# RWKV features and scan: idle products ahead of waits, decay jobs in head pairs, bonus products between the gates', three VectorE operations per key chunk, and one GpSimd operation fewer per unit

## What is computed

```python
u = _centred_token_shift(u, mu).astype(f32)
r, k, v, wd, ad, gd = jnp.split(u, splits, axis=-1)
w = -jax.nn.softplus(-(w0 + jnp.einsum('bldr,drc->bldc', jnp.tanh(wd), w2))) - 0.5
decay = jnp.exp(-jnp.exp(w))
a = jax.nn.sigmoid(a0 + jnp.einsum('bldr,drc->bldc', ad, a2))
g = jax.nn.sigmoid(gd) @ g2
kk = (k * k_k).reshape(B, L, H, N)
kk = kk / jnp.maximum(jnp.sqrt(jnp.sum(kk * kk, axis=-1, keepdims=True)), 1e-12)
k_dir = k[:, :, None, :] * (1.0 + (a - 1.0) * k_a)
...
_, ys = lax.scan(_rwkv7_step, S0, seq)          # the scan, both directions
...
bonus = jnp.sum(r_h[:, :, None] * k_h * r_k, axis=-1, keepdims=True)
y = y + (jnp.sum(bonus, axis=2) * v_h).reshape(B, L, D_RWKV)
y = y * g
return y.astype(out_dtype) @ w_o
```

## Time and profile before

| | before |
|---|---|
| median of 3 runs (lowest, highest) | 3057.55 us (3047.7, 3060.89) |
| the profiled execution: its own time | 3049.9 us |
| its span, first to last instruction | 3048.1 us |
| PE busy | 2815.7 us, 92% of the span |
| DVE, ACT, POOL busy | 1561.3, 871.8, 376.5 us |
| clock granted to TensorE, mean over the span | 0.961 of full speed |
| the features stage | about 508.5 to 551.2 us of the span |
| the scan | about 551.2 to 841 us |

### The profile page before, as it was taken

How to read it: one execution, slowest core, us unless ns; L and a number is a source line. 1 busy time by engine, 2 the same in 40 slices (tenths; PEclk the granted TensorE clock), 3 DMA queues, 4 the chain that set the end, 5 groups by cost and what they waited for, 6 DMA issues and landing times. The chain is left out here.

```text
span 3048.1 us, 40943 instructions
## 1 busy us (share of the span) xinstructions
PE 2815.7 (92%) x17635; PEld 2216.8 (73%) x17635; DVE 1561.3 (51%) x2138; ACT 871.8 (29%) x1119; POOL 376.5 (12%) x356
## 2 busy tenths in 40 slices
PE   7999999788899999999999999799999669999997
PEld 6888876577765777788887854578887545688886
DVE  5555454566676734555545317463354545463342
ACT  3222234211134223322213423332222334432221
POOL 1111010211110001111100001121121100120110
PEclk9999999899999999999999988899999879999999
DMA  4555531000030023355544210223343200222321
GB/s 146 169 169 162 163 114 50 2 3 3 3 119 14 28 83 97 110 163 169 164 161 126 89 43 0 70 69 105 110 145 104 56 31 29 70 83 97 97 97 55
DMA packets 267444, 272.05 MB, mean 89 GB/s; under 512 B 12751, under 2 KB 248246, under 8 KB 267071
## 3 DMA queue, kind: packets, MB, share of 16 engines
q1 hardware_dynamic: 251904, 207.57, 22.0%
q0 software_dynamic: 15360, 61.87, 6.2%
HBM read 267.32 MB, written 2.10 MB: 88 GB/s over the span
## 5 line engine op out<-in xcount | busy, mean ns | idle before, releaser
L915 DVE TENSOR_TENSOR mix_wl<-ring_raw,mix_wh 128x2048 fp32r<-128x2048 f32 (+2 forms) x66 | 153.1, 2320 | 220.1 <-ACT mix_wh L807 220.0
L707 PE MATMUL mix_ps<-h_mix_hi,mix_wh 128*128 128x512 f32 x624 | 244.1, 391 | 0.0
L709 PE MATMUL mix_ps<-h_mix_lo,mix_wh 128*128 128x512 f32 x624 | 242.8, 389 | 0.0
L807 ACT ACTIVATE mix_wh<-ring_raw 128x2048 fp32r<-128x2048 f32 (+2 forms) x66 | 117.6, 1782 | 212.5 <-PE mix_ps L713 162.1
L707 PE MATMUL ffn_ps<-h_rw_hi,ffn_wh 128*128 128x512 f32 x448 | 175.3, 391 | 0.0
L709 PE MATMUL ffn_ps<-h_rw_lo,ffn_wh 128*128 128x512 f32 x448 | 174.3, 389 | 0.0
L915 DVE TENSOR_TENSOR mlp_wl<-ring_raw,mlp_wh 128x2048 fp32r<-128x2048 f32 (+1 forms) x38 | 96.7, 2545 | 131.5 <-ACT mlp_wh L807 131.5
L915 DVE TENSOR_TENSOR mlp_wl<-mlp_raw,mlp_wh 128x2048 fp32r<-128x2048 f32 x36 | 93.2, 2589 | 133.3 <-ACT mlp_wh L807 133.3
L713 PE MATMUL mix_ps<-h_mix_hi,mix_wl 128*128 128x512 f32 x624 | 154.2, 389 | 0.0
L707 PE MATMUL mlp_ps<-view,mlp_wh 128*128 128x512 f32 x384 | 150.1, 391 | 0.0
L709 PE MATMUL mlp_ps<-view,mlp_wh 128*128 128x512 f32 x384 | 149.5, 389 | 0.0
(11 more groups left out here) (589 smaller groups left out, 6210.4 us busy)
## 6 DMA issues: line engine op xcount, KB each, us to landing
ring_raw<-in_mlp_w SPq DMA_DIRECT2D x32, 1024.0 KB, 5.3
mlp_raw<-in_mlp_w SPq DMA_DIRECT2D x32, 1024.0 KB, 5.2
ffn_sraw<-in_ada_w POOLq DMA_DIRECT2D x34, 768.0 KB, 5.1
ffn_raw<-in_ffn_w_gu SPq DMA_DIRECT2D x44, 512.0 KB, 5.1
ring_raw<-in_ffn_w_gu SPq DMA_DIRECT2D x44, 512.0 KB, 4.8
mix_sraw<-in_ada_w POOLq DMA_DIRECT2D x22, 768.0 KB, 5.0
ring_raw<-in_w_in SPq DMA_DIRECT2D x14, 1024.0 KB, 5.2
ring_raw<-in_a_w_in SPq DMA_DIRECT2D x12, 1024.0 KB, 5.2
```

What stands on the lines that cost most here:

```text
L707: nc.tensor.matmul(ps[:, it.banks[t], :], w(h, k, t), xh[:, k, :], start=it.first and k == it.k0, stop=False)
L709: nc.tensor.matmul(ps[:, it.banks[t], :], w(h, k, t), xl[:, k, :], start=False, stop=False)
L807: nc.scalar.activation(slot(wh, it), slot(raw, it), ACT.Copy).then_inc(hi_ready, 1)
L915: nc.vector.tensor_tensor(slot(wl, it), slot(raw, it), slot(wh, it).bitcast(F32), ALU.subtract)\
```

## The change

It has six parts.

1. In the features, PE issues six `keep_clock` products between the first four jobs and the spread, once the square root is ready (`n_root`).
2. The decay jobs go chunk by chunk, both directions next to each other, as the `a` jobs did already.
3. Each bonus product stands behind its chunk's gate job and not behind all jobs.
4. DVE makes r * r_k * k for all chunks (`krr`) ahead of the reciprocal, and then has three operations per chunk, not four: s = a_fwd + a_bwd - 2; s * k_a * krr; 2 * krr + that.
5. A table `rest` = 1 - k_a is made once, and GpSimd's factor is a * k_a + rest in one pass: the operation over all 512 columns that added 1.0 (L1944) goes, with its wait.
6. At the scan's start PE waits for `logs_done`, issues six `keep_clock` products, makes unit 0's `begin`, and issues six more.

```diff
@@ rwkv_features
+        krr = sb("krr", [P, RT, L])
+        kd, rk = sb("kd", [P, L]), sb("rk", [P, 2, L])
@@
         jobs = [("a", d, c) for c in range(RT) for d in range(2)] + \
-               [("w", d, c) for d in range(2) for c in range(RT)] + [("g", 0, c) for c in range(RT)]
+               [("w", d, c) for c in range(RT) for d in range(2)] + [("g", 0, c) for c in range(RT)]
@@ tensor
                 if n == 4:
+                    pe.wait_ge(n_root, 1)
+                    keep_clock(nc, e, pn[:, RT - 1, :], 6)
                     pe.wait_ge(spread_in, 16)
                     pe.wait_ge(inv_ready, 1)
@@
-            for c in range(RT):
-                pe.wait_ge(rk_ready, c + 1)
-
-                pe.wait_ge(kk_ready, c + 1)
-                nc.tensor.matmul(pn[:, c, :], e.heads[:, :], rk[:, c % 2, :], start=True, stop=True)\
-                    .then_inc(b_done, 1)
+                if kind == "g":
+                    pe.wait_ge(rk_ready, c + 1)
+                    pe.wait_ge(kk_ready, c + 1)
+                    nc.tensor.matmul(pn[:, c, :], e.heads[:, :], rk[:, c % 2, :], start=True, stop=True)\
+                        .then_inc(b_done, 1)
@@ vector
             pick_heads(nc, e, dve, pick, picked)
+            ka = COL["rw_k_a"]
+            nc.vector.tensor_scalar(grown, e.cols[:, ka:ka + RT], -1.0, 1.0, ALU.mult, ALU.add)
+            for c in range(RT):
+                st.mark(nc.vector.scalar_tensor_tensor(krr[:, c, :], r[:, c, :], col(e, "rw_r_k", c), k[:, c, :],
+                                                       ALU.mult, ALU.mult))
+            dve.wait_ge(steps, st.n)
             dve.wait_ge(n_root, 1)
@@
-                then(nc.vector.tensor_scalar(kd[:, 0, :], kd[:, 0, :], col(e, "rw_k_a", c), 2.0,
-                                             ALU.mult, ALU.add))
-                then(nc.vector.tensor_tensor(kd[:, 0, :], kd[:, 0, :], k[:, c, :], ALU.mult))
+                then(nc.vector.scalar_tensor_tensor(kd[:, :], kd[:, :], col(e, "rw_k_a", c), krr[:, c, :],
+                                                    ALU.mult, ALU.mult))
                 if c >= 2:
                     dve.wait_ge(b_done, c - 1)
-                nc.vector.scalar_tensor_tensor(rk[:, c % 2, :], kd[:, 0, :], col(e, "rw_r_k", c), r[:, c, :],
-                                               ALU.mult, ALU.mult).then_inc(rk_ready, 1)
+                nc.vector.scalar_tensor_tensor(rk[:, c % 2, :], krr[:, c, :], 2.0, kd[:, :], ALU.mult, ALU.add)\
+                    .then_inc(rk_ready, 1)
@@ rwkv_scan, gpsimd
                 for c in range(RT):
-                    ins = nc.gpsimd.tensor_scalar(kd[:, c, :], au[:, c, :], -1.0, col(e, "rw_k_a", c), ALU.add, ALU.mult)
+                    ins = nc.gpsimd.tensor_scalar(kd[:, c, :], au[:, c, :], col(e, "rw_k_a", c), col_at(rest, c),
+                                                  ALU.mult, ALU.add)
                 ins.then_inc(kd_done, 1)
-                pool.wait_ge(kd_done, 4 * u + 1)
-                nc.gpsimd.tensor_scalar(kd[:, :, :], kd[:, :, :], 1.0, None, ALU.add).then_inc(kd_done, 1)
-                pool.wait_ge(kd_done, 4 * u + 2)
+                pool.wait_ge(kd_done, 3 * u + 1)
@@ tensor
+            pe.wait_ge(logs_done, 1)
+            keep_clock(nc, e, pc[0], 6)
             begin(0)
+            keep_clock(nc, e, pc[0], 6)
```

More of the change, by code:

```diff
@@ L1721, in load_spread, with rwkv_features @@
     return sp.dma_start(spread[:, :, :], I["c_sel"].rearrange("k (h p) -> k h p", h=2 * RT)[:, :, 0:CH])
-def rwkv_features(nc, e, I, rkv, lora, lw, a, g, kk, bonus, tables):
+def rwkv_features(nc, e, I, rkv, lora, lw, a, g, kk, bonus, grown, tables):
     r, k, v = rkv[:, 0:RT, :], rkv[:, RT:2 * RT, :], rkv[:, 2 * RT:3 * RT, :]
@@ L1740, in rwkv_features @@
         pick, spread = sb("pick", [P, RT, 2 * RT]), sb("spread", [2 * RT, 2 * RT, CH])
-        kd = sb("kd", [P, 2, L])
-        rk = sb("rk", [P, 2, L])
+        krr = sb("krr", [P, RT, L])
+        kd, rk = sb("kd", [P, L]), sb("rk", [P, 2, L])
         ps = pb("ps", [P, 4, L])
@@ L1845, in _ @@
                 dve.wait_ge(taken, 2 * c + 2)
-                then(nc.vector.scalar_tensor_tensor(kd[:, 0, :].rearrange("p (q i) -> p q i", i=QL), a[:, 0, :, c, :], -2.0,
+                then(nc.vector.scalar_tensor_tensor(kd[:, :].rearrange("p (q i) -> p q i", i=QL), a[:, 0, :, c, :], -2.0,
                                                     a[:, 1, :, c, :], ALU.add, ALU.add))
-                then(nc.vector.tensor_scalar(kd[:, 0, :], kd[:, 0, :], col(e, "rw_k_a", c), 2.0,
-                                             ALU.mult, ALU.add))
-                then(nc.vector.tensor_tensor(kd[:, 0, :], kd[:, 0, :], k[:, c, :], ALU.mult))
+                then(nc.vector.scalar_tensor_tensor(kd[:, :], kd[:, :], col(e, "rw_k_a", c), krr[:, c, :],
+                                                    ALU.mult, ALU.mult))
                 if c >= 2:
                     dve.wait_ge(b_done, c - 1)
-                nc.vector.scalar_tensor_tensor(rk[:, c % 2, :], kd[:, 0, :], col(e, "rw_r_k", c), r[:, c, :],
-                                               ALU.mult, ALU.mult).then_inc(rk_ready, 1)
+                nc.vector.scalar_tensor_tensor(rk[:, c % 2, :], krr[:, c, :], 2.0, kd[:, :], ALU.mult, ALU.add)\
+                    .then_inc(rk_ready, 1)
                 dve.wait_ge(rk_ready, c + 1)
@@ L1871, in level_columns, with rwkv_scan @@
     return t.rearrange("p m (g two b) -> p (m g) two b", two=2, b=b)[:, :, odd, :]
-def rwkv_scan(nc, e, I, rkv, lw, a, kk, y, g, bonus, reset, scan_mask, levels):
+def rwkv_scan(nc, e, I, rkv, lw, a, kk, y, g, bonus, rest, reset, scan_mask, levels):
     r, k, v = rkv[:, 0:RT, :], rkv[:, RT:2 * RT, :], rkv[:, 2 * RT:3 * RT, :]
@@ L2225, in scale @@
                 elif part == 2:
-                    dve.wait_ge(kd_done, 4 * u + 4)
+                    dve.wait_ge(kd_done, 3 * u + 3)
                     if u >= 2:
@@ L2451, in rwkv_branch @@
         reset, mask, levels = sb("reset", [P, L]), sb("mask", [P, 2, P]), sb("levels", [P, 2 * LEVELS + 1, CH])
+        rest = sb("rest", [P, RT])
         tables = [(reset[:, :], I["c_reset"]), (mask[:, :, :], I["c_scan"].rearrange("p (d t) -> p d t", d=2)),
                   (levels[:, :, :], I["c_levels"].rearrange("p (k t) -> p k t", t=CH))]
-        rwkv_features(nc, e, I, rkv, y, lw, a, g, kk, bonus, tables)
-        rwkv_scan(nc, e, I, rkv, lw, a, kk, y, g, bonus, reset, mask, levels)
+        rwkv_features(nc, e, I, rkv, y, lw, a, g, kk, bonus, rest[:, :], tables)
+        rwkv_scan(nc, e, I, rkv, lw, a, kk, y, g, bonus, rest, reset, mask, levels)
     return bonus, g
```

## The result

| | before | changed |
|---|---|---|
| median (lowest, highest) of 7 runs each | 3057.52 us (3047.7, 3060.89) | 3037.65 us (3029.84, 3040.91) |
| the profiled execution: its own time | 3049.9 us | 3036.13 us |

The ratio is 0.9937, with a 95% interval of 0.9922 to 0.9951. Measured once more (after_again, five runs against nine of before), the same kernel came to 3038.32 against 3051.3 us, 0.9950 (0.9933 to 0.9968). The forecast was 3042 (3030 to 3053) and a gain of 13.5; the medians give 19.9 and 13.0.

A forecast was written before the change was run, and what follows sets the result against it. PE sets the features' end; in the scan its waits for `scaled` and `x` lie on the path. Gains 6.1 + 2.1 + 5.3 = 13.5 give 3036.4 us from the profiled execution, 3044 from the median; said 3042, range 3030 to 3053.

The forecast's parts named there:

- first rival: Whole kernel: the clock gains more, through the shorter wait for x in the units; about 3035 us, chance 0.22.
- spread behind idle products: Features, PE: with six idle products in the gap the spread takes about 4.6 us, not 7.16; gain 2.4.
- second four `a` jobs: Features, PE behind the spread: left at the lower clock, gain 0, up to 1.4 if the clock does not fall.
- decay jobs: Features, PE: eight jobs with alternating row halves take 4.3 us instead of 5.72; gain 1.4 (0.9 to 1.7).
- gates and bonus products: Features, PE: 12.65 us without a stall instead of 14.35, since `rk` is early; gain 1.7.
- tail: End of features, DVE: only the last product with v follows PE, 1.33 us becomes 0.7; gain 0.6.
- up to the reciprocal (`krr`): Features: four `krr` operations, 3.0 us, fit in DVE's idle 5.60 ahead of `n_root`; cost 0.
- scan's start: Scan's first unit: 0.5 from GpSimd's lost pass and 1.6 from the idle products' clock; gain 2.1 (-1 to 4.7).
- units 1 to 6: Scan: `kka` ends before L2248, which falls to 0.68 us; `x` comes 0.88 earlier six times, gain 5.3.
- second rival: Features: GpSimd blocks DVE for a whole pass, fourth `krr` ends at 517.85; gain 10.8, 3047 us, chance 0.10.
- slack of 0.45: Scan's units 1 to 6: GpSimd's four small operations may cost 0.1 us more each with their second table before it goes.
- third rival: Scan's units: small operations slower, `kka` still meets L2248; gain 8.2, 3050 us, or 3053 if idle products cover nothing; chance 0.13.

The follow-up runs named there:

- a_early_kd: Changed kernel with GpSimd's four unit 0 operations made in the features, unit 1's waiting for unit 0's x, idle products 4 and 5; 3035.88 us, 0.9942 of before.
- a_jobs_old: Changed kernel with the decay jobs by direction again, equal row halves next to each other; single time 3039.14 us.
- a_four_ops: Changed kernel with VectorE's four operations per chunk again and no r * r_k * k ahead of the reciprocal; single time 3036.43 us.
- a_pool_old: Changed kernel with GpSimd's five old operations per unit, the pass that adds 1.0 being back; 3046.08 us, 0.9987 of before.
- b_pool_new: Kernel before with GpSimd's new operations alone, the small table made by VectorE in the features; 3049.13 us, 0.9988 of before.
- b_pool_late: Kernel before with GpSimd's old operations, the next unit's waiting for x of the present one (started in place of scaled); 3046.95 us, 0.9985 of before.
- a_no_idle_feat: Changed kernel without the features' six idle products, those at the scan's start staying; no time given, 30.39 us from reciprocal to scan against 28.44 changed.
- a_no_idle: Changed kernel without its eighteen idle products, in the features and at the scan's start; 3038.68 us, 0.9964 of before.

## Why the prediction was right

The time lies in the range and the gain has the forecast's sign; the terms held less well than their sum. The first medians' gain, 19.9, lies beyond the forecast's 10 to 17, in a part (over 15.3) to which I had given 0.40; the second measurement's 13.0 and the traces' 16.1 lie within 10 to 17. By time alone 3037.65 is as near to the first rival's 3035 as to 3042; the lengths of the units decide between them. The trace of before is that of a fast execution, 7.6 under the median. Step by step, in us gained:

| step | said | the traces |
|---|---|---|
| spread behind idle products | 2.4 | 3.5 |
| second four `a` jobs | 0 | 0.5 |
| decay jobs | 1.4 | 0.5 |
| gates and bonus products | 1.7 | 2.2 |
| tail | 0.6 | 0.6 |
| up to the reciprocal (`krr`) | 0 | -0.7, of which `krr`'s -0.3 |
| scan's start | 2.1 | 2.5 |
| units 1 to 6 | 5.3 | 5.3, and 1.6 of the clock's |
| sum | 13.5 | 16.1 |

The **spread** was sized by the group norm's row, in which the clock fell half way; here it held to the end, and the next job starts 3.6 after the spread does, the upper bound that I gave and did not take. It fell behind the spread instead, in the `a` jobs, and stayed down into the first decay jobs.

**Decay jobs**: these eight took 5.26 and not the 4.3 that I had sized, and the clock is the small part of the miss. In a_early_kd it stood at 1.00 through all of them, and they still took 5.10, from 525.84 to 530.94: seven steps of 0.58, each job starting 0.05 behind the end of one of ScalarE's operations, and 1.05 from the last job to the first gate. So ScalarE, which frees the buffers of `ps` every 0.58, sets the pace of the pairs. I had that case, 4.8 if it binds throughout, and did not take it, because the four buffers let PE run ahead; it binds all the same. By direction TensorE's own 0.72 is the slower of the two, which is why pairing is worth 0.8 (a_jobs_old) and not 1.4. **Gates and bonus products** are 12.12 and not 12.65, as the products next to a bonus product follow after 0.96 and not 1.06.

**krr**: GpSimd's pass did not block VectorE. The four took 3.08, 0.77 each, beside GpSimd's, and were done 3 us ahead of the square root; the second rival, by which they would end at 517.85, fell. By the rule of the Trainium skill that stands beside it ("SBUF — State Buffer", section "SBUF: two separate sides") one operation has the shared ports for its whole instruction. In this case that holds for two operations that read two tensors each: L2232 at 1.76 beside GpSimd's product, L2260 at 1.75, and the other way round GpSimd's product at 1.77, which began 0.06 behind L2228. It does not hold beside GpSimd's passes over one tensor: there GpSimd is the slower by 1.1 in all, and VectorE at most by 0.27. But what I put at 0 was not quite that. From GpSimd's first operation of the stage to the reciprocal it took 7.64, before 6.91, of which the maximum's 0.26 is shown (a_four_ops); the rest is the clock in the sums of squares, which made this length anything from 6.9 to 8.7 in the runs.

**Scan's start**: GpSimd lost the pass of 1.50 and the first `scaled` came only 0.42 earlier, 0.5 being said. The reason given, a new meeting, holds, but it was to stretch VectorE's operation, and GpSimd's are stretched as well: its two products took 0.93 more together beside L2228 and L2232, its four small operations 0.25 more. The idle products hold nothing up and gave 1.2 to 2.1; I had counted 1.6. a_early_kd takes away both GpSimd's chain and the meetings, and the 3.6 that these still cost came back.

**Units**: shown on both sides, by a_pool_old and b_pool_new, and by b_pool_late, which removes the meeting and no operation. The slack of 0.45 was used up to 0.32 by the second table (1.74 for 1.42), and the third rival did not come. The first rival was argued from the shorter gap, and that argument fell: a_pool_old has the long gap and the least time at the lower clock. That the changed kernel's trace has 6.8 us less of it than before's is 1.6 of its 16.1, and not shown to be due to the change; where the clock falls differs between executions. The 19.9 of the first medians may hold more of such luck and the 13.0 of the second less; that is not shown.

## What to carry to other kernels

When an operation is twice as long at one place as at another, look at what the other engine runs in that window: here 0.88 us in each of six units came from one GpSimd product that began 0.25 us before a VectorE operation with two SBUF inputs, and moving it was worth about as much as all idle products together. Before taking a faster order of products for a gain, look at the engine that takes the results out: here ScalarE's 0.58 per job held the pairs, which by TensorE alone would take 0.50. Idle products pay in front of a short wait if they end before what they wait for, and at a second place they become the bound as soon as the wait shrinks. A change worth 0.5% in parts of 0.1% is read from lengths between two fixed operations in the trace; times of whole executions told only the sum.

## What the runs showed of the hardware

The granted clock fell to 0.50 at places that differ between executions of like code: in the kernels whose code is the same from the scan's second unit on, with waits of about 2.05 before each unit, some units show it and some don't (13.6 to 20.4 us in all). One such stretch in a unit of the scan cost 0.6 to 0.8 us; at the spread, in a_no_idle_feat against a_no_idle, 1.6. PE was busy through all 7.1 us of the spread in a_no_idle, and at the lower level throughout; in the changed kernel the same spread began at 1.00 behind idle products, and the clock fell 0.7 us behind its end. ScalarE took a 128x512 result out of PSUM every 0.58 us (a_early_kd). GpSimd's operation with two column tables took 0.435 us for 128 columns against 0.355 with one. And a GpSimd pass over one tensor beside VectorE's operations with two did not hold VectorE up by more than 0.27 us, but became slower itself, 7.33 for 6.21.
